# Two transformer blocks on one Trainium2 core: half-size products in the first block's input projection, a ring of 11 slots that becomes 6, and another order of the first block's weights

## The reference, cut to what matters

```python
mod = silu(c) @ w_ada + b_ada                    # 6 vectors of 1024: shift, scale, gate, twice
h = rms_norm(x, norm1_g) * (1 + scale1) + shift1
proj = h @ w_in                                  # 256 x 1024 @ 1024 x 4096
q, k, v, u, z_gate = split(proj)                 # 512, 512, 512, 512, 2048
y_attn = attention(q, k, v) @ w_branch_attn      # 8 heads, causal, a learned bias by distance
y_pool = pool_mixer(u) @ w_branch_pool
g_attn, g_pool = split(sigmoid(z_gate + b_gate))
x = x + gate1 * ((g_attn * y_attn + g_pool * y_pool) @ w_out)
x = x + gate2 * hier_moe(rms_norm(x, norm2_g) * (1 + scale2) + shift2)   # 32 experts, 2 of them per token
```

## Time and profile before

| what | value |
| --- | --- |
| median of 3 runs | 1366.16 us (1366.12 to 1367.88) |
| the profiled execution | 1367.74 us, of which the span from first to last instruction is 1366.0 us |
| TensorE busy | 1330.3 us (97%) |
| VectorE busy | 614.0 us (45%) |
| ScalarE busy | 297.7 us (22%) |
| moved by DMA | 364.59 MB, mean 267 GB/s |
| mean granted TensorE clock | 0.992 |
| chain that ended last | TensorE 68%, DMA 10% |

### The profile page before, as it was taken

The page is one execution under the profiler, slowest core; times in us unless marked ns, Lnnn a source line. Parts: engine busy times, 40 slices in busy tenths (PEclk is TensorE's granted clock), DMA queues, the critical chain, the costliest instruction groups (busy, mean ns, idle before and its releaser), DMA issues.

```text
span 1366.0 us, 20544 instructions
## 1 busy us (share of the span) xinstructions
PE 1330.3 (97%) x8538; PEld 997.6 (73%) x8538; DVE 614.0 (45%) x1398; ACT 297.7 (22%) x589; POOL 7.8 (1%) x18
## 2 busy tenths in 40 slices
PE   7999999999999999888999999999999999999997
PEld 5888886444334443333588889999998878999996
DVE  6456254111100100100468738674545773867454
ACT  2234102112112112111243611220014362122000
POOL 0000000000000000000000000000000000000000
PEclk8999999999999999999999999999999999999999
DMA  9998785999999999999954144444444414444410
GB/s 393 378 404 319 315 358 195 422 412 421 422 423 421 421 423 421 424 422 419 422 190 146 60 155 176 163 170 171 166 165 144 147 60 155 166 174 160 180 63 32
DMA packets 52096, 364.59 MB, mean 267 GB/s; under 512 B 6161, under 2 KB 6465, under 8 KB 8994
## 3 DMA queue, kind: packets, MB, share of 16 engines
q1 hardware_dynamic: 49392, 355.49, 65.6%
q10 hardware_dynamic: 1890, 5.04, 1.3%
q0 software_dynamic: 720, 2.72, 0.5%
HBM read 359.02 MB, written 2.11 MB: 264 GB/s over the span
## 4 chain that ended last, share of the span: by engine, by line
PE 68%; DMA 10%; DVE 0%; DVEq 0%; issue 0%; ACT 0%
PE bank L1156 27%; PE bank L877 14%; PE bank L630 12%; DMA ring<-in_weights 6%; DMA ringx<-in_weights 4%; PE bank L642 3%; PE bank L888 3%; PE bank L1301 2%; PE bank L1092 2%; PE bank L1205 1%; PE bank L1256 1%; PE bank L1282 1%; PE bank L1269 1%; PE bank L925 0%; PE bank L862 0%; PE bank L1066 0%
## 5 line engine op out<-in xcount | busy, mean ns | idle before, releaser
L630 PE MATMUL bank<-h,ring 128*128 128x256 f32 x832 | 183.8, 381 | 0.1
L877 PE MATMUL bank<-ring,cst 128*64 128x512 f32 x608 | 174.7, 594 | 6.9 <-DMA ring<-in_weights 4.2
L630 PEld LDWEIGHTS bank<-h,ring 128*128 128x128 f32 x832 | 156.9, 190 | 22.7 <-issue 1.5
L877 PEld LDWEIGHTS bank<-ring,cst 128*64 128x64 f32 x608 | 54.5, 137 | 96.8 <-issue 95.8
L2063 DVE TENSOR_TENSOR act<-act,bank 128x512 f32<-128x512 f32 (+1 forms) x17 | 11.1, 656 | 240.5 <-PE bank L877 240.5
L1156 PE MATMUL bank<-hid,ring 128*128 128x128 f32 x912 | 115.6, 275 | 0.0
L1156 PE MATMUL bank<-h,ring 128*128 128x128 f32 x896 | 113.8, 275 | 0.0
L1156 PEld LDWEIGHTS bank<-hid,ring 128*128 128x128 f32 x912 | 108.6, 192 | 0.0
L1156 PEld LDWEIGHTS bank<-h,ring 128*128 128x128 f32 x896 | 107.0, 192 | 0.1
L1156 PE MATMUL bank<-sq,ring 128*128 128x128 f32 x720 | 95.1, 275 | 0.0
L877 PE MATMUL bank<-ringx,cst 128*64 128x512 f32 x232 | 86.2, 596 | 2.6 <-DMA ring<-in_weights 2.6
(11 more groups left out here) (386 smaller groups left out, 1802.8 us busy)
## 6 DMA issues: line engine op xcount, KB each, us to landing
ring<-in_weights SPq DMA_DIRECT2D x250, 1024.0 KB, 10.5
ringx<-in_weights SPq DMA_DIRECT2D x45, 1024.0 KB, 23.0
spare<-in_weights SPq DMA_DIRECT2D x18, 1024.0 KB, 18.9
pool_a<-in_weights SPq DMA_DIRECT2D x9, 1024.0 KB, 19.4
x<-in_weights SPq DMA_DIRECT2D x9, 1024.0 KB, 23.6
ring<-in_weights SPq DMA_DIRECT2D x4, 512.0 KB, 23.6
spare<-in_weights SPq DMA_DIRECT2D x4, 512.0 KB, 19.1
x<-in_x SPq DMA_DIRECT2D x1, 1024.0 KB, 4.9
```

The source lines that it names most:

```text
L630: ins = e.matmul(u.ap[:, 0:S], w[:, k * width + j * P:k * width + (j + 1) * P], acts[:, k, :], start=k == 0, stop=k == kc - 1)
L877: ins = e.matmul(g.bank[bank][ex * SLOTS:(ex + 1) * SLOTS, :], stat(m, ex), pair[ex][:, m * 512:(m + 1) * 512], start=first and m == 0, st ...
```

## The change

What it does, in the order of the code:

- **Tile order and slots.** The first 22 tiles use a ring of 11 slots (RF = 11), tiles 22 to 47 a ring of 6 (RS = 6, SHRINK = 22). Slot 11 and the first spare slot become buffers for sums of weights, the second spare slot a buffer for differences of h. Five expert tiles go to slots 6 to 10 right after tile 27; the other seventeen early ones come behind tile 47. Behind i8 the order of tiles is i9 a13 i10 i11 a14 i12 i13 a15 i14 i15 a16 b0 a17 b1 a18 b2 a19 a20 b3 a21 b4 a22 b5 a23 b6 b7.
- **Half-size products.** i4 to i15 are multiplied by seven products (`pe_first_seven`), i4 to i7 with the activations as the stationary operand.
- **VectorE.** It forms the differences and the sums of i4 and i5 ahead of the angles (`dve_angles`), and then per tile an ada tile, the recombination, and the sums of the tile after next. In the gate stage the scores of the attention stand ahead of the sums, and an ada tile comes at every second gate.
- **ScalarE.** Copies of first products; the sigmoids run from and to the gate buffer, five tiles of them behind gate 5. Two function tables are loaded ahead of their use.
- **Start.** The eight squares are summed by eight matmuls, without VectorE; the spread of c comes ahead of four unread matmuls. The bias table's product moves ahead of i0, its transfers to the very start, and GpSimd sends it on after `h_shifted` 8.

```diff
+RF, RS = 11, 6
+SHRINK = 2 * RF
+FIRST_SLOTS = (*range(RS, RF), RF, *SPARE, R + 3, R + 5, R + 2, AHEAD, R, R + 1, 2, 3, 4, 5, R + 4, 0, 1, KEPT)
...
-        n = t % R if t < T_EXP else expert_slot(t - T_EXP) if t < T_LAYERS else (t - T_LAYERS) % RL
+        n = (t % RF if t < SHRINK else (t - SHRINK) % RS) if t < T_EXP else expert_slot(t - T_EXP) if t < T_LAYERS else (t - T_LAYERS) % RL
...
+FIRST_ORDER = ("a4 a0 i0 a5 a1 i1 a6 a2 i2 a7 a3 i3 a8 i4 a9 i5 a10 i6 a11 i7 a12 i8 i9 a13 i10 i11 a14 i12 i13 a15 i14 i15 "
+               "a16 b0 a17 b1 a18 b2 a19 a20 b3 a21 b4 a22 b5 a23 b6 b7").split()
...
+    first = [T_EXP + n for n in FIRST_TILES]
+    amid = SHRINK + RS
+    for t in [*range(amid), *first[:RF - RS], *range(amid, T_EXP), *first[RF - RS:]]:
...
     for j in range(4):
-        w = g.filled(e, in_tile(4 + j))
-        pe_tokens(e, g, ("vu", j), w, g.h, ready)
-        g.owed += 1
+        pe_first_seven(e, g, j)
...
     for j in range(8):
-        w = g.filled(e, in_tile(8 + j))
-        for jj in range(2):
-            pe_chunk(e, g, ("gate", 2 * j + jj), w, jj, 256, KC, g.h, ready)
-        g.owed += 1
+        pe_first_seven(e, g, 4 + j)
         pe_attention_step(e, g, A, j + 1)
...
     dve_ada(e, g, 8)
+    e.wait_ge(s["h_shifted"], KC)
+    dve_differences(e, g, g.h, g.first_diff[1:], g.first_diff[0])
+    dve_first_sums(e, g, 0)
+    dve_first_sums(e, g, 1)
     dve_angles(e, g)
...
+        dve_ada(e, g, 9 + j)
+        dve_tokens_seven(e, g, j)
+        dve_first_sums(e, g, j + 2)
     dve_scores(e, g, A, 0)
     for j in range(8):
-        dve_ada(e, g, 12 + j)
+        dve_seven(e, g, ("gate", j), 5 + j, g.gate[:, 2 * j * S:(2 * j + 2) * S], g.first_a, g.first_pair)
         if j < 3:
             dve_scores(e, g, A, j + 1)
+        if j < 6:
+            dve_first_sums(e, g, 6 + j)
+        if j % 2 == 1:
+            dve_ada(e, g, 13 + j // 2)
```

More of the change, by code:

```diff
@@ L143 @@
 UPS = 14
+BIAS_AFTER = 8
 SEVENS = UPS + 15
@@ L596, in pe_norm_added, with pe_norm_first @@
         ins = e.matmul(u.ap[:, 0:S], g.c("ones"), sq[:, k, :], start=k == 0, stop=k == last)
+    g.last(u, ins)
+def pe_norm_first(e, g):
+    u = g.take(e, ("ss", 0))
+    for k in range(KC):
+        e.wait_ge(g.s["squares"], k // 2 + 1)
+        ins = e.matmul(u.ap[:, 0:S], g.c("ones"), g.sq[:, k, :], start=k == 0, stop=k == KC - 1)
     g.last(u, ins)
@@ L726, in part @@
             g.owed += 1
-    pe_norm_added(e, g, 0)
+    pe_norm_first(e, g)
+    u = g.take(e, ("row",))
+    e.wait_ge(g.s["tab_in"], 48)
+    g.last(u, e.matmul(u.ap[0:HEADS, 0:NB_ROW], g.rb[0:BUCKETS, 0:HEADS], g.tab[0:BUCKETS, :], start=True, stop=True))
     pe_unread(e, g, 5)
@@ L1141, in pe_seven @@
     w = g.filled(e, layer_tile(l, 18 + i))
[L1142 to L1145, removed]
+    acts = token_quarters(g.h if i < UPS else g.hid[:, 8 * b:8 * b + 8, :])
+    diffs = g.h_diff if i < UPS else g.hid_diff[b]
     if i >= UPS and b == 3:
-        t1 = g.t1_last
+        acts[0][1] = g.t1_last
     if b == 0:
@@ L1397, in act_first @@
     for j in range(8):
[L1398 to L1401, removed]
+        g.evac(e, *(("gate", j - 1, 0) if j else ("vu", 3, 0)))
+        act_first_product(e, g, ("gate", j), g.first_a)
+        if j < 5:
+            act_attention_step(e, g, A, j + 1)
+        for n in range(j) if j == 5 else (j - 1,) if j > 5 else ():
+            act_gate(e, g, n)
+    act_gate(e, g, 7)
     for gr in range(4):
@@ L2319, in dve_differences, with dve_tokens_seven, dve_seven @@
     e.tensor_tensor(t4, b21, t2, ALU.subtract).then_inc(g.s["diff_ready"], 1)
-def dve_seven(e, g, key, n, out):
+def dve_tokens_seven(e, g, j):
+    to = (g.v3 if j < 2 else g.u3)[:, :, (j % 2) * 256:(j % 2 + 1) * 256]
+    left, right = to[:, :, 0:P], to[:, :, P:2 * P]
+    two = lambda a: a.rearrange("p (n t) -> p n t", n=2)
+    twice = lambda a: a.unsqueeze(1).to_broadcast([P, 2, P])
+    one, pair, key = g.first_a, g.first_pair, ("vu", j)
+    x = g.full(e, *key, 0)
+    e.wait_ge(g.s["first_product"], j + 1)
+    g.read((*key, 0), e.tensor_tensor(left, twice(one), two(x[:, P:3 * P]), ALU.add))
+    g.evac(e, *key, 0)
+    y = g.full(e, *key, 1)
+    g.step.up(e.tensor_tensor(two(pair), twice(left[:, 1, :]), two(y[:, 0:2 * P]), ALU.add))
+    g.after(e)
+    e.tensor_tensor(left[:, 1, :], pair[:, 0:P], y[:, 2 * P:3 * P], ALU.add)
+    e.tensor_tensor(right[:, 0, :], pair[:, P:2 * P], y[:, 3 * P:4 * P], ALU.add)
+    g.read((*key, 1), e.tensor_tensor(right[:, 1, :], pair[:, P:2 * P], y[:, 0:P], ALU.add))
+def dve_seven(e, g, key, n, out, one=None, pair=None):
+    one, pair = (g.one_a, g.pair_a) if one is None else (one, pair)
     two = lambda a: a.rearrange("p (n t) -> p n t", n=2)
```

131 lines of the change are left out of this document (77 added, 54 removed).

## The result

The changed kernel takes 1371.1 us (median of 6 runs, 1369.1 to 1373.4) against 1366.1 (median of 6). The ratio is 1.0037, 95% interval 1.0026 to 1.0048: slower by 0.37%. Forecast: 1371.2, slower. The profiled execution took 1370.57 and spans 1368.8.

A forecast was written before the change was run, and what follows sets the result against it. Transfers bound the kernel until the last expert tile lands: T = 156.3 plus 507.3 gives 663.6, 5.0 us later than 658.55, so 1366.16 + 5.0 = 1371.2 us. Range 1360.5 to 1375.9, likeliest case 1367.5 to 1374.

The forecast's parts named there:

- The start, +0.7: Before i4: i0 done 0.7 us later through the bias table's eviction on VectorE; no shift taken from the squares.
- T: Start of the branches on TensorE; 154.77 us in the kernel before, forecast 156.3, 1.5 later.
- i5 lands at 57.0: First block: i4 waits for i0's slot, goes at 46.7, lands at 51.6; i5 two tiles later, letting VectorE begin.
- 40.4 us of VectorE from there to gate 1: First block: sums, angles, four tiles at 6.95 us, an attention step and gate 0 put together, ending at 97.4.
- Gate 1 to T, 51.4 + 0.7, then the small product: Gates and attention 51.4 us, 0.7 wait in step 3; last gate ends 149.5, small product's sum done 154.4.
- Half-size products save TensorE 8.4: Twelve tiles at 6.25 us instead of 6.97: 8.4 to 8.6 us less TensorE time if nothing else is late.
- b7 at T + 31.3: Last tile ahead of the seventeen early expert tiles, waiting for VectorE to take a21: issued at T + 31.3 us.
- 188 tiles and 6.7 for the write: T + 507.3: From T + 32.5, 188 tiles take 468.1 us, plus 6.7 around the write of x; last expert tile lands.
- The new queue costs 3.5: Break-even at T = 151.3: TensorE must win 3.5 us in the first block only to pay for the queue.
- The clock falls: Rival: TensorE's waits around i6 and attention step 1 drop its clock, costing 1.5 to 3 us; 1374, chance 0.12.
- the seventeen tiles: Early expert tiles now behind b7, most formerly sent in pauses; each counted at 2.49 us of saturated transfers.

The follow-up runs named there:

- same_again: The changed kernel itself, unaltered, measured once more against the kernel before: 1371.49 us, ratio 1.0034.
- squares_old: early_both with the first norm's squares added up by VectorE and summed once by TensorE, as in the kernel before: 1358.01 us, ratio 0.9936.
- full_early: Full-size products and the old start, with early_both's tile order and four expert tiles ahead of b2: 1367.05 us, ratio 1.0002 to the kernel before.
- x4_oldmath: The kernel before with only the new queue (tile order, slots, places of conditioning tiles); full-size products, old start: 1369.02 us, ratio 1.0019.
- write_alone: The changed kernel with the write of x issued by ScalarE on its own queue instead of by SP: 1368.05 us, ratio 1.0015 to the kernel before.
- x1_angles: The changed kernel with VectorE's angles moved ahead of the sums of i4: 1369.24 us, ratio 1.0019 to the kernel before.
- x2_queue: The changed kernel with four of the seventeen late expert tiles issued ahead of b2 instead of behind b7: 1368.73 us, ratio 1.0015 to the kernel before.
- x3_order: The changed kernel with i4 and i5 queued ahead of a8 and a9, and a8 taken behind the two sums: 1369.51 us, ratio 1.0025 to the kernel before.
- early_both: The changed kernel with i5 queued earlier, a8 behind the two sums, a16 behind the router's sum, four expert tiles ahead of b2: 1359.67 us, ratio 0.9946.
- early_only: early_both without the four expert tiles moved ahead of b2: 1361.83 us, ratio 0.9965 to the kernel before.

## Why the prediction was right

- *The start, +0.7.* Wrong sign. The first product of i4 began at 53.49 and, in same_again, 54.94 (forecast 55.7). VectorE then waited for i4 and i5, but the start still counts, through i0's slot: between these two traces the first instruction on the sum, i4's issue, i5's landing and T all move by 1.2 to 1.4 us. The lead over before (13.08 for that instruction, against 15.30) is not the squares' doing: with the old squares it stands at 13.53 (squares_old) and 13.94 (full_early).
- *i5 lands at 57.0.* Measured 58.37. i4 went at 44.62 (forecast 46.7), since i0 was used up sooner, but landed 6.9 later and i5 another 6.8. The two misses offset each other, 2.1 less for the issue and 3.5 more for the transfers; that is luck.
- *40.4 us of VectorE from there to gate 1.* Measured 38.1 (58.37 to 96.4), with 0.5 of idle time in it. Each of my durations held some tenths of a gap: a tile of the stage took 6.45, not 6.95. Gate 1 at 96.68, forecast 97.4: 2.3 too many here against 1.4 too few ahead of it.
- *Gate 1 to T, 51.4 + 0.7, then the small product.* Measured 52.0 (96.68 to 148.67), and 1.32 of waiting for the router's sum, as said. T = 155.63 and 156.97 in two traces, forecast 156.3.
- *Half-size products save TensorE 8.4.* Where next to nothing holds them they save 7.0: from the start of i4's products to T it is 92.1 us in squares_old (53.46 to 145.54) and 99.1 in full_early (55.59 to 154.66), both with the old squares, the same order and the four tiles. T and the time differ by more, 9.1 and 9.0, since i4 began 2.1 earlier too; the moved bias product is in that, and so is the scatter of the start. In the changed kernel none of it arrives: its T, 155.63 and 156.97, is no earlier than the 154.68 of x4_oldmath, with the same queue and full-size products.
- *b7 at T + 31.3.* Measured T + 31.2. *188 tiles and 6.7 for the write: T + 507.3.* Measured T + 506.0 and 506.3: the sum was 1.0 to 1.3 too large. The last tile was used at 661.60 and 663.27, forecast 663.6. (The 2.0 us of the Trainium skill, DMA: Bandwidth & Descriptors, section Anatomy of one DMA, which the prediction sets beside its 2.5 for a pause, is given there for transfers that GpSimd issues; this one was SP's.)
- *The new queue costs 3.5.* Measured 2.8 (x4_oldmath), and 3.0 come back with write_alone.
- *The clock falls* was a rival with 0.12. It happened in the wait of 4.65 inside i6: granted clock 0.50 from 72 to 76.

```profile
72.00:74.00 2.00, 1.78 (x8) 1.78 (x9) 2.00 (x4) 0.00 (x0) 0.00 (x0) 0.50 1.02 426
```

It cost nothing there, since VectorE set the pace; in x1_angles, where it fell at gate 1, it took 1.7. In five kernels with waits in this stage (the changed one, x1_angles, x2_queue, x3_order, write_alone) the clock fell once each between 66 and 100, and in early_both, whose only wait there is 0.57, not at all. The Trainium skill's rule on the swinging clock (TensorE: Matmul & The Clock Gate, section on the second failure mode) is about short idles between groups. x1_angles agrees, where the fall came behind waits of 0.56, 0.94 and 1.03; in the changed kernel it came behind one long wait, which that section does not describe.

One step of the reasoning was too simple though the sum was right. I took the seventeen tiles as what must be paid, and each tile brought forward as 2.49 won. The runs show two gates: F at T + 79, and the landing of the write. The last tile is used 423 to 425 us behind the later of them. In the changed kernel that is the write, 2 us behind F, and one tile more is left (171 for 170): for its T its end is 3.4 later than where F is the gate (506.0 against 502.6). The kernel before has F as its gate and yet 503.8: in its trace, a long one, the experts took a microsecond more than in the others with F. The prediction took its marks from that trace. So the agreement of the medians, 1371.1 against 1371.2, is closer than the reasoning earned: terms of 1 to 3.5 us missed both ways.

## What to carry to other kernels

When transfers bound a later stage, ask which event lets the queue go on for good. Whatever is issued before it costs only if it delays that event, and bringing it forward pays only up to the next such event. A write whose landing frees a buffer shouldn't stand at the end of a long queue: another queue gave back 3.0 of 5.0 us by itself. And when arithmetic is moved from the bound engine to a helper, look first for the tile that lets the helper begin: here the products' saving of 7 us arrived once i4 and i5 no longer stood behind i0's slot (and a8 and a16 had moved behind what is urgent).

## What the runs showed of the hardware that I had not expected

A tile of 1 MB takes 2.49 us in the saturated stretch; here the two tiles behind i4, a9 and i5, took 6.8 to land, 3.4 each. The page of queues for 44 to 60 us of the changed kernel (packets, MB, share of the engines' time):

```profile
q1 hardware_dynamic: 551, 4.09, 64.3%
q0 software_dynamic: 371, 1.45, 29.9%
```

The load of the bias table, on GpSimd's queue, moves a quarter of the bytes, and the weights share the engines with it. In x3_order, where i5 took 9.9 to land, the engines moved 283 GB/s in 46 to 48 at a busy share of 0.99, against 423 in the experts. Whether a later load of the bias table brings i5 forward was not tried in the changed kernel, but x4_oldmath shows what it may be worth. It has the same queue, and loads the table only after i5 has landed. The row of i5's issue in the page of DMA issues (KB, us from issue to landing), of x4_oldmath and then of the changed kernel:

```profile
ring<-in_weights SPq DMA_DIRECT2D x1, 1024.0 KB, 8.9
```

```profile
ring<-in_weights SPq DMA_DIRECT2D x1, 1024.0 KB, 12.9
```

So the early table, a part of the change itself, costs i5 some 4 us, an estimate from these two rows.

The squares' eight matmuls, the same instructions at about the same time, took 3.62 us in early_only and 4.66 in early_both, which differ in the queue only a hundred microseconds later. The kernels with the old start scatter too: six of the unread matmuls take 5.43 us in the kernel before and 2.86 in full_early, though the granted clock reads 1.00 in both. T moves with the start from run to run. Why it differs stays open; the change put the squares' matmuls on the path and so let this into the time.
